# Attention outputs of a head kept and normed four blocks at a time, convolution taps given out one by one, the gate projected last, the query copies on ScalarE

## The chip, the core and the metric

The kernel runs on one core of one Trainium2 chip. The metric is the time of one execution in device microseconds (us). The core has TensorE (PE in the profile, PEld for its weight loads), VectorE (DVE), ScalarE (ACT) and GpSimd (POOL); SyncE (SP) issues the DMAs. The engines run their own instruction lists in order and meet only at semaphores.

## What is computed

One layer of a hybrid decoder on 1024 tokens and 16 meta tokens, model width 1024, in float32. The normed input is projected once, and three groups use it: differential attention (4 heads), a short gated convolution and a Mamba-2 scan (4 groups of 4 heads). The parts of the reference that the change touches:

```python
u = rmsnorm(h, norm_w[layer])
proj = jnp.einsum('bld,de->ble', u, w_in[layer])
(q, k, v, g_attn, c_b, c_c, c_h, g_conv, z, xbc, dt) = jnp.split(proj, IN_SPLIT_POINTS, axis=-1)
y_attn = diff_attention_branch(q, k, v, ...) * jax.nn.silu(g_attn)
y_conv = short_conv_branch(c_b, c_c, c_h, sconv_w[layer]) * jax.nn.silu(g_conv)
y_ssm = ssd_branch(z, xbc, dt, ...)
h = h + jnp.einsum('ble,ed->bld', concat(y_attn, y_conv, y_ssm), w_out[layer])

# in diff_attention, a block of 128 queries of one head, two maps m = 0, 1
s = jnp.einsum('bqhmd,bkhmd->bhmqk', qi, k) * scale
p = jax.nn.softmax(jnp.where(mask, s, MASK_VALUE), axis=-1)
a = p[:, :, 0] - lam * p[:, :, 1]
o = jnp.einsum('bhqk,bkhe->bqhe', a, v)
# and after it
o = rmsnorm(o, sub_norm_w) * (1.0 - lam_init)
```

## The kernel before

The work is done head by head. A loop runs over heads 0 to 2 (`BODY`), head 3 is written out (`LAST`), and a prologue (`AHEAD`) norms the input and projects the first head's q, k and v. After the heads come the output projection (L1360) and the final norm.

**Projections.** A head has 14 weight tiles of 128 columns (`TILES`): q, k, v, the attention gate (TG), the convolved tiles xs 0, xs 1, B and C (TXS0, TXS1, TB, TC), two z tiles, and four of the short convolution (TCB, TCC, TCH, TGC). Float32 is kept by splitting each weight and input into a high and a low part: three matmuls for each product (high by high, high by low, low by high; L1353). A tile is loaded by SP ("load"), copied to its high part by ScalarE (L807) and its low part made by GpSimd (L738), both in step "split"; two tiles, TZ1 and TCB (`SHARED`), have their low part made half by GpSimd and half by VectorE (L1097). A tile is projected in three pieces of 348 columns, each in two halves of 12 matmuls. Pieces go in turn to two banks of PSUM, and a bank is used again when the engine that empties it gives it back (`bank_free`).

**Order.** All engines walk through one list of steps, written by `schedule()`. Each engine takes from it the steps in which it has a part, so the list sets the order of every engine. Step s of the attention stage (s = 0 to 8) does for block s: scores of map 0, exponential, scores of map 1, exponential, mix. In the same step it does for block s-1: "turn" (TensorE transposes the mixed probabilities, VectorE and ScalarE copy them back), "values" (times v) and "o_norm". "attn_out" is for block s-2. Between them `fill()` gives out half pieces of projections as cover.

**A block's output before.** VectorE scales and clips the 128x128 result into `o_n` (L1200, L1201). ScalarE sums its squares (L908), VectorE makes the mean (L1205, L1206), GpSimd the power -1/2 (L725), VectorE the normed block (L1208). TensorE transposes it, and VectorE multiplies it with the gate (L1212, which gives `attn_ok`). `o_n` has room for one block, and the turn of the next block waits for the last of these:

```python
eng.wait_ge(a_m_ok, it * QB + a + 1)
eng.wait_ge(attn_ok, it * QB + a + 1)
for n in range(a + 1):
    turn(t_ps[n // 4][:, ...], prob[0][:, ...])
```

**Taps.** The four convolved tiles get four taps each on VectorE (L1157, three times L1159), a tanh on ScalarE (L882) and a gate on VectorE (L1168). The `half_pieces()` function puts each at a fixed half piece after its tile. The parameters of a head are gathered by ten small VectorE operations (L1105 to L1117) with the first convolved tile.

**Queries.** ScalarE scales the two high parts out of PSUM (L852, L853). VectorE subtracts them from the product (L1127, L1129) and copies each high part to the other half of the partitions (L1128, L1130). The second copy gives the bank back.

Of the kernel before, what the change touches and what calls it, by code (L numbers as in the profile page):

```python
# [15 lines left out]
P = 128  # L16
D = 1024
T = 1024
META = 16
# [31 lines left out]
(TQ, TK, TV, TG, TXS0, TXS1, TB, TC, TZ0, TZ1, TCB, TCC, TCH, TGC) = range(NT)  # L51
# [23 lines left out]
def half_pieces(tiles, d):  # L75
# [3 lines left out]
    tail = [[] for _ in range(6)]  # L79
    places = units + tail  # L80
    n = 0
    for t in tiles:
# [8 lines left out]

        if TXS0 <= t <= TC:
            for tap in range(4):
                places[n - 1 + tap].append(("taps", (t, tap), d))
            places[n + 3].append(("gate_taps", t, d))
        if t == TGC:
            for part in range(5):
                places[n - 1 + part].append(("conv", part, d))
    return units, tail
# [44 lines left out]
def schedule(last):  # L144

# [8 lines left out]
    def ahead(name, t, d):  # L154
        add(name, t % NT, d + t // NT)

    def filler(units, slots):
# [8 lines left out]
        return fill  # L166

    def emit(unit):
        for name, arg, d in unit:
            if name in ("load", "split"):  # L170
                ahead(name, arg, d)
            else:
                add(name, arg, d)


    units, tail = half_pieces([TG, TXS0, TXS1, TB, TC], 0)
    units[-1] += [("split", TZ1, 0), ("load", TCB, 0), ("load", TCC, 0)]
    fill = filler(units, sum(ATT_FILL))
    for s in range(QB + 1):
        f = [ATT_FILL[s] * w for w in ATT_SPLIT]  # L180
# [15 lines left out]
        if s >= 1:  # L196
            add("values", s - 1)
        if s < QB:
            add("mix", s)
        if s >= 1:  # L200
            add("o_norm", s - 1)
        fill(f[2])

    emit(tail[0])
    add("z", 1)
    emit(tail[1])
    add("z", 2)
    emit(tail[2])
    emit(tail[3])
    add("z", 3)  # L210
    add("attn_out", QB - 1)
    add("store_attn")
    add("z", 4)
# [1385 lines left out]
```

## Time and profile before

| | |
|---|---|
| runs of the kernel before | 1181.78 us median of 3 (1181.15 to 1184.64) |
| the profiled execution: its own time | 1181.38 us |
| its span, first to last instruction | 1179.7 us |
| mean granted TensorE clock | 0.985 |
| TensorE busy | 1086.4 us, 92% |
| VectorE busy | 647.6 us, 55% |
| ScalarE, GpSimd busy | 381.9 us, 32%; 293.0 us, 25% |

A granted clock of 1.0 is 2.4 GHz and 0.5 is 1.2 GHz. The rows of matmuls overlap: one lasts until its result is written, while the next starts well before. In the rows further down, `[1.22 <-DVE y_a L1208]` means that the engine was idle for 1.22 us before this instruction, and that line 1208 of VectorE ended the wait.

### The profile page before, as it was taken

To read this page: it belongs to the slowest core of one execution; us is meant where nothing else is said; L and a number is where in the kernel's file an instruction comes from. 1 tells how busy PE (TensorE), PEld (TensorE's weight loads), DVE (VectorE), ACT (ScalarE), POOL (GpSimd) and SP (SyncE) were. 2 spreads that over 40 slices of the span, in tenths; PEclk is the share of its full clock that TensorE was granted. 3 is DMA by queue.
4 is the path that set the end of the run, shared out by engine and by line. 5 is a ranking of instruction groups with operands and counts; after the bars stand their busy time and mean duration, and the time that the engine had idled before them with its cause. 6 is when DMAs were issued, how large, how long until landed. Compare 5 with 4: busy or idle time off the path is not lost.

```text
span 1179.7 us, 18700 instructions
## 1 busy us (share of the span) xinstructions
PE 1086.4 (92%) x6681; PEld 1002.8 (85%) x6681; DVE 647.6 (55%) x1329; ACT 381.9 (32%) x840; POOL 293.0 (25%) x255
## 2 busy tenths in 40 slices
PE   4889989999999899998998999999989998999997
PEld 3679888899888889998888899999888997888885
DVE  6453666645546766465467664654675646325324
ACT  5223333232333332233333322333332324323324
POOL 5311120332211203331112033311121332432433
PEclk9989999999999999999999999999999999999999
DMA  5101001311130013111300131112011222963423
GB/s 185 36 22 55 18 20 36 90 46 45 54 91 19 20 35 99 41 41 54 91 18 20 35 99 41 41 54 90 19 36 55 74 80 79 343 226 122 157 80 143
DMA packets 91876, 85.89 MB, mean 73 GB/s; under 512 B 4478, under 2 KB 78316, under 8 KB 91788
## 3 DMA queue, kind: packets, MB, share of 16 engines
q1 hardware_dynamic: 91788, 84.70, 22.6%
q8 instruction: 57, 0.93, 0.3%
q14 instruction: 31, 0.25, 0.1%
HBM read 72.03 MB, written 12.66 MB: 72 GB/s over the span
## 4 chain that ended last, share of the span: by engine, by line
PE 43%; issue 35%; DVE 8%; POOL 8%; DMA 2%; ACT 2%; SPq 1%; POOLq 0%; DVEq 0%; ACTq 0%
PE ps L1353 19%; PE ps L1360 15%; POOL w_lo L738 5%; PE ps L1515 3%; PE ps L1345 2%; POOL small L725 2%; DMA acum_b<-acum_scratch 2%; PE ps L1529 1%; DVE lm_buf L1231 1%; DVE work L1159 1%; PE ps L1531 1%; PE ps L1535 1%; ACT w_hi L807 1%; DVE work L1188 1%; DMA work<-in_x 1%
## 5 line engine op out<-in xcount | busy, mean ns | idle before, releaser
L1353 PE MATMUL ps<-u_hi,w_hi 128*128 128x348 f32 x1152 | 393.6, 342 | 22.9 <-DVE q_hl L1130 14.7
L1353 PE MATMUL ps<-u_lo,w_hi 128*128 128x348 f32 x1152 | 375.0, 326 | 0.0
L1353 PE MATMUL ps<-u_hi,w_lo 128*128 128x348 f32 x1152 | 374.2, 325 | 0.0
L1353 PEld LDWEIGHTS ps<-u_hi,w_hi 128*128 128x128 f32 x1152 | 221.4, 192 | 32.3 <-issue 11.2
L1353 PEld LDWEIGHTS ps<-u_lo,w_hi 128*128 128x128 f32 x1152 | 220.9, 192 | 0.7
L1353 PEld LDWEIGHTS ps<-u_hi,w_lo 128*128 128x128 f32 x1152 | 220.5, 191 | 0.0
L738 POOL TENSOR_TENSOR w_lo<-w_raw,w_hi 128x1024 fp32r<-128x1024 f32 (+1 forms) x56 | 129.2, 2308 | 190.5 <-ACT w_hi L807 190.5
L725 POOL TENSOR_TENSOR small<-small,m_half 128x1 f32<-128x1 f32 (+1 forms) x81 | 54.6, 674 | 463.4 <-DVE small L1206 294.9
L1360 PE MATMUL ps<-w_hi,u_hi 128*128 128x512 f32 x256 | 99.8, 390 | 4.2 <-DVE u_lo L996 3.3
L1360 PE MATMUL ps<-w_hi,u_lo 128*128 128x512 f32 x256 | 101.6, 397 | 0.0
L1360 PE MATMUL ps<-w_lo,u_hi 128*128 128x512 f32 x256 | 101.4, 396 | 0.0
L1345 PE MATMUL ps<-ident,work 128*128 128x128 f32 (+2 forms) x401 | 64.3, 298 | 36.3 <-DVE conv_u L1212 19.1
L996 DVE TENSOR_TENSOR u_lo<-q_hl,u_hi 128x1024 fp32r<-128x1024 f32 x32 | 43.0, 1348 | 88.2 <-ACT u_hi L791 88.1
L1180 DVE TENSOR_REDUCE small<-ps 128x1 f32<-128x144 f32 (+7 forms) x64 | 49.5, 774 | 71.7 <-PE ps L1466 67.9
L1345 PEld LDWEIGHTS ps<-ident,work 128*128 128x128 f32 (+2 forms) x401 | 49.7, 149 | 44.5 <-issue 32.6
L729 POOL TENSOR_TENSOR w_lo<-w_raw,w_hi 128x512 fp32r<-128x512 f32 x32 | 59.1, 1853 | 106.6 <-ACT w_hi L795 106.5
L1515 PE MATMUL ps<-w_hi,u_hi 128*128 128x256 f32 x256 | 74.0, 289 | 6.1 <-DVE w_lo L1097 3.8
L1515 PE MATMUL ps<-w_lo,u_hi 128*128 128x256 f32 x256 | 71.9, 281 | 0.0
L1515 PE MATMUL ps<-w_hi,u_lo 128*128 128x256 f32 x256 | 71.8, 280 | 0.0
L896 ACT ACTIVATE work<-ps,small 128x144 f32<-128x144 f32 (+7 forms) x64 | 48.0, 749 | 66.1 <-DVE small L1180 66.1
L791 ACT CAST u_hi<-q_hl 128x1024 fp32r<-128x1024 f32 x32 | 33.5, 1051 | 99.1 <-PE ps L1360 84.3
L1360 PEld LDWEIGHTS ps<-w_hi,u_hi 128*128 128x128 f32 x256 | 49.1, 192 | 16.1 <-issue 5.0
(209 smaller groups left out, 1693.4 us busy)
## 6 DMA issues: line engine op xcount, KB each, us to landing
w_raw<-in_w_in SPq DMA_DIRECT2D x56, 512.0 KB, 3.9
q_hl<-y_scratch SPq DMA_DIRECT2D x32, 512.0 KB, 3.7
acum_b<-acum_scratch SPq DMA_DIRECT2D x32, 256.0 KB, 4.0
w_raw<-in_w_out SPq DMA_DIRECT2D x32, 256.0 KB, 4.3
work<-in_x SPq DMA_DIRECT2D x8, 512.0 KB, 3.8
y_scratch<-ys SPq DMA_DIRECT2D x8, 512.0 KB, 3.3
work<-in_x SPq DMA_DIRECT2D x4, 1024.0 KB, 8.8
out<-work SPq DMA_DIRECT2D x8, 512.0 KB, 3.0
```

The lines of the kernel that those rows point to most:

```text
L725: return eng.tensor_tensor(to[0:rows_, n:n + 1], of[0:rows_, n:n + 1], m_half[0:rows_, :], ALU.pow)
L729: eng.tensor_tensor(wo_lo[:, b, :], wo_raw[:, b, :], wo_hi[:, b, :].bitcast(F32), ALU.subtract).then_inc(wo_lo_ok, 1)
L738: eng.tensor_tensor(w_lo[:, a % 2, ks, :], w_raw[:, a % 2, ks, :], w_hi[:, a % 2, ks, :].bitcast(F32), ALU.subtract).then_inc(w_lo_ok, 1)
L791: eng.copy(y_hi[:, b, :], y_raw[:, b, :]).then_inc(y_hi_ok, 1)
L807: eng.copy(w_hi[:, b, :, :], w_raw[:, b, :, :]).then_inc(w_hi_ok, 1)
L896: eng.activation(prob[m][:, 0:nk], s_ps[:, 0:nk], ACT.Exp, bias=mx[:, m:m + 1], accum_out=psum_e[:, s % 2, m:m + 1]).then_inc(exp_ok, 1)
L996: eng.tensor_tensor(y_lo[:, b, :], y_raw[:, b, :], y_hi[:, b, :].bitcast(F32), ALU.subtract).then_inc(y_lo_ok, 1)
L1180: eng.tensor_reduce(mx[:, m:m + 1], s_ps[:, 0:nk], AX.X, ALU.max, negate=True).then_inc(max_ok, 1)
L1345: return eng.transpose(dst, src, ident[0:n, 0:n])
L1353: ins = eng.matmul(dst, w[:, k, 0:m], u[:, k, cols], start=(k == 0 and n == 0), stop=(k == KD - 1 and n == 2))
L1360: ins = eng.matmul(ps[:, t, :], y[:, b, t * P:(t + 1) * P], w[:, b, :], start=(first and m == 0), stop=(last and m == 2), skip_group_check ...
L1515: ins = eng.matmul(pb[p % 2][:, 0:GW], u[:, k, ca:cb], w[:, :, k, :], start=(k == 0 and n == 0), stop=(k == KD - 1 and n == 2))
```

## The change

- **Attention outputs.** `o_n` has room for eight blocks (it lies in `conv_y`, which is free during attention). Steps "o_norm" and the eight "attn_out" go. Instead "o_mean" and "o_scale" treat four blocks in one operation each, after blocks 3 and 7. Two "attn_out" steps transpose four blocks into a bank of their own and gate 512 columns at once; the first stands behind the last turn, the second behind z 3. The turn of a block waits for `o_c_ok`, the clip of the block before, and no longer for `attn_ok`.
- **Order of tiles.** The gate tile TG comes after TC, so the parameters move to the first step of a head.
- **Taps.** Taps, gates of tiles and the five steps of the short convolution go to a list, `jobs`. `spare()` gives out one job at a place, at three places of each step.
- **Shared low halves.** For TZ1 and TCB ScalarE copies the high part in two halves. VectorE makes the first low half as soon as the first is there and GpSimd the second. TensorE waits for the second only at its second half of work.
- **Query copies.** ScalarE makes them; the bank is given back after VectorE's second subtraction. The first scores wait for `q_twice_ok`.
- **Meta rows.** `a_meta` and `v_meta` have 128 rows, zero below the 16 in use, so the last matmul of "values" has 128 rows too.

```diff
-TILES = [(C_Q, P), (C_K, P), (C_V, P), (C_G, P), (C_XS, GW), (C_XS + P, GW), (C_B, P), (C_C, P),
+TILES = [(C_Q, P), (C_K, P), (C_V, P), (C_XS, GW), (C_XS + P, GW), (C_B, P), (C_C, P), (C_G, P),
...
         if TXS0 <= t <= TC:
-            for tap in range(4):
-                places[n - 1 + tap].append(("taps", (t, tap), d))
-            places[n + 3].append(("gate_taps", t, d))
+            jobs += [(n, ("taps", (t, tap), d)) for tap in range(4)] + [(n, ("gate_taps", t, d))]
...
+                while jobs and jobs[0][0] <= state[0] - 7:
+                    emit([jobs.pop(0)[1]])
                 emit(units[state[0]])
                 state[0] += 1
...
+        def spare(n):
+            while n > 0 and jobs and jobs[0][0] <= state[0]:
+                emit([jobs.pop(0)[1]])
+                n -= 1
+        return fill, spare
...
         if s < QB:
             add("scores", (s, 0))
-        if s >= 2:
-            add("attn_out", s - 2)
         fill(f[0])
+        if s < QB:
+            spare(ATT_SPARE[0])
...
+        if s == QB:
+            add("split", TZ1)
+            add("load", TCB)
+            add("load", TCC)
+            add("attn_out", 0)
...
-        if s >= 1:
-            add("o_norm", s - 1)
+        if s == 6:
+            add("o_scale", 0)
         fill(f[2])
...
-ATT_SPLIT = (.3, .3, .4)
+ATT_SPLIT = (.2, .4, .4)
+ATT_LAST = (1, 0, 0)
+ATT_SPARE = (1, 1, 1)
+SCAN_SPARE = (1, 1, 1)
...
@@ ScalarE @@
+                        if a in SHARED:
+                            eng.copy(w_hi[:, b, 0:KD // 2, :], w_raw[:, b, 0:KD // 2, :]).then_inc(w_half_ok, 1)
+                            eng.copy(w_hi[:, b, KD // 2:KD, :], w_raw[:, b, KD // 2:KD, :]).then_inc(w_hi_ok, 1)
...
                             eng.mul(q_hi[1][QK:P, to], src[QK:P, of], QK ** -0.5).then_inc(qk_hi_ok, 1)
+                            eng.wait_ge(qk_hi_ok, it * 2 * PIECES + tc + 1)
+                            eng.copy(q_hi[0][QK:P, to], q_hi[0][0:QK, to].bitcast(F32))
+                            eng.copy(q_hi[1][0:QK, to], q_hi[1][QK:P, to].bitcast(F32)).then_inc(q_twice_ok, 1)
...
@@ VectorE @@
-                            eng.tensor_copy(q_hi[0][up, to], q_hi[0][lo, to].bitcast(F32))
...
-                            eng.tensor_copy(q_hi[1][lo, to], q_hi[1][up, to].bitcast(F32)).then_inc(done, 1)
...
+                    elif step == "o_scale":
+                        ns = slice(4 * a, 4 * a + 4)
+                        eng.wait_ge(o_rs_ok, it * 2 + a + 1)
+                        own(eng, eng.tensor_tensor(o_rs[:, ns], o_rs[:, ns], o_fit[:, ns], ALU.mult))
+                        eng.tensor_tensor(o_n[:, ns, :], o_n[:, ns, :], o_rs[:, ns].unsqueeze(2).to_broadcast([P, 4, P]), ALU.mult).then_inc(o_n_ok, 1)
                     elif step == "attn_out":
+                        eng.wait_ge(o_tr, it * 2 + a + 1)
+                        cols = slice(META + 4 * P * a, META + 4 * P * (a + 1))
+                        eng.scalar_tensor_tensor(gate[:, cols], ot_ps[a][:, :], a_norm[:, 0:1], gate[:, cols],
...
@@ TensorE @@
-                        eng.wait_ge(attn_ok, it * QB + a + 1)
+                        eng.wait_ge(o_c_ok, it * QB + a + 1)
```

The first place is VectorE's list around step 5 of a head, before: the mean and norm of block 4 (L1205 to L1208), two taps (L1159), the reduction of the next scores (L1180), the gate of block 3 (L1212) and a third tap.

```order
L1205 TENSOR_SCALAR small<-small 128x1
L301 REGISTER_ALU
L1206 TENSOR_SCALAR small<-small 128x1
L1208 TENSOR_SCALAR y_a<-y_a,small 128x128
L1159 SCALAR_TENSOR_TENSOR work<-lm_buf,par_cw,work 128x1044
L301 REGISTER_ALU
L1159 SCALAR_TENSOR_TENSOR work<-lm_buf,par_cw,work 128x1044
L301 REGISTER_ALU
L1176 REGISTER_ALU
L1180 TENSOR_REDUCE small<-ps 128x1
L1212 SCALAR_TENSOR_TENSOR conv_u<-ps,a_norm,conv_u 128x128
L1159 SCALAR_TENSOR_TENSOR work<-lm_buf,par_cw,work 128x1044
```

The same step in the changed kernel, from its mix of block 5 (L1206) on: a tap (L1177), the reduction (L1198), a tap, and the copy of the turned probabilities (L1211).

```order
L1206 SCALAR_TENSOR_TENSOR work<-work,small 128x784
L1177 SCALAR_TENSOR_TENSOR work<-work,par_cw 128x1044
L307 REGISTER_ALU
L1194 REGISTER_ALU
L1198 TENSOR_REDUCE small<-ps 128x1
L1177 SCALAR_TENSOR_TENSOR work<-work,par_cw 128x1044
L307 REGISTER_ALU
L1210 REGISTER_ALU
L1211 COPY conv_g<-ps 128x512
```

Norm and gate of a block have left this place, and the taps stand one at a time between the operations of the softmax.

The second place is VectorE's list for the first query piece of the next head, before: subtraction, copy, subtraction, copy, then a step of the short convolution (L1220).

```order
L1126 ISA
L1127 SCALAR_TENSOR_TENSOR q_hl<-ps,q_hl 64x332
L1128 CAST q_hl<-q_hl 64x332
L1129 SCALAR_TENSOR_TENSOR q_hl<-ps,q_hl 64x332
L1130 CAST q_hl<-q_hl 64x332
L1220 SCALAR_TENSOR_TENSOR conv_y<-conv_u,par_sw,conv_y 128x1024
```

The changed kernel's list there, with the second piece's subtractions and then the convolution step (L1244).

```order
L1146 ISA
L1147 SCALAR_TENSOR_TENSOR q_hl<-ps,q_hl 64x332
L1148 SCALAR_TENSOR_TENSOR q_hl<-ps,q_hl 64x332
L1146 REGISTER_ALU
L1147 SCALAR_TENSOR_TENSOR q_hl<-ps,q_hl 64x348
L1148 SCALAR_TENSOR_TENSOR q_hl<-ps,q_hl 64x348
L1244 SCALAR_TENSOR_TENSOR conv_y<-conv_u,par_sw,conv_y 128x1024
```

The copies have gone to ScalarE, and the convolution step stands a piece later.

The third place is VectorE's list at the start of a head, before: the reduction of the first scores and then the copy of the turned values (L1171).

```order
L1180 TENSOR_REDUCE small<-ps 128x1
L1170 REGISTER_ALU
L1171 COPY conv_b_s<-ps 128x512
L1137 ISA
L1138 ISA
L1139 SCALAR_TENSOR_TENSOR conv_u<-th_piece,ps 128x348
```

The changed kernel's list there, from the last of the small parameter operations to the copy of the turned values (L1189).

```order
L1134 COPY small<-d_bc 128x4
L1135 REGISTER_ALU
L1135 COPY sg<-stat 128x180
L307 ISA
L1137 MEMSET lm_buf 128x3
L307 REGISTER_ALU
L1188 REGISTER_ALU
L1189 COPY conv_b_s<-ps 128x512
L1194 REGISTER_ALU
L1198 TENSOR_REDUCE small<-ps 128x1
```

The parameters stand ahead of that copy now, and the gate's product (L1139) has left this place.

## Rows read from the trace of the kernel before

**Rows 1.** The page, part 1: busy time, share and count of each engine

```profile
PE 1086.4 (92%) x6681; PEld 1002.8 (85%) x6681; DVE 647.6 (55%) x1329; ACT 381.9 (32%) x840; POOL 293.0 (25%) x255
```

**Rows 2.** TensorE's waits: us in total, times, longest

```profile
PE ps L1345 <- DVE conv_u L1212: 19.1, 13, 2.0
...
PE ps L1345 <- DVE y_a L1208: 8.0, 16, 1.2
...
PE ps L1353 <- DVE q_hl L1130: 14.7, 7, 5.5
...
PE ps L1515 <- DVE w_lo L1097: 3.8, 3, 1.3
...
PE ps L1353 <- POOL w_lo L738: 3.4, 3, 1.1
```

**Rows 3.** Timeline, head 1, step 5: start us, us, engine, line

```profile
389.11 2.37 POOL L738 TENSOR_TENSOR w_lo<-w_raw,w_hi 128x1024 fp32r<-128x1024 f32 x1
389.18 2.38 DVE L1208 TENSOR_SCALAR y_a<-y_a,small 128x128 f32<-128x128 f32 x1 [0.67 <-POOL small L725]
...
391.62 0.33 PE L1345 MATMUL ps<-ident,y_a 128*128 128x128 f32 x1 [1.22 <-DVE y_a L1208]
...
393.36 0.32 PE L1353 MATMUL ps<-u_lo,w_hi 128*128 128x348 f32 x1
...
393.52 0.32 PE L1353 MATMUL ps<-u_hi,w_lo 128*128 128x348 f32 x1
...
395.33 0.34 DVE L1212 SCALAR_TENSOR_TENSOR conv_u<-ps,a_norm,conv_u 128x128 f32<-128x128 f32 x1
...
395.82 0.96 PE L1345 MATMUL ps<-ident,work 128*128 128x128 f32 x7 [1.98 <-DVE conv_u L1212]
```

**Rows 4.** Timeline, head 2's query pieces, end of head 1's pass

```profile
527.98 2.62 POOL L738 TENSOR_TENSOR w_lo<-w_raw,w_hi 128x1024 fp32r<-128x1024 f32 x1 [1.56 <-ACT w_hi L807]
...
528.73 0.50 DVE L1127 SCALAR_TENSOR_TENSOR q_hl<-ps,q_hl 64x332 fp32r<-64x332 f32 x1 [0.37 <-ACT q_hl L853]
...
529.24 1.55 DVE L1128 CAST q_hl<-q_hl 64x332 fp32r<-64x332 f32 x1
...
530.16 0.46 ACT L853 ACTIVATE q_hl<-ps 64x348 fp32r<-64x348 f32 x1
...
531.71 0.43 PE L1353 MATMUL ps<-u_hi,w_hi 128*128 128x348 f32 x1 [1.83 <-DVE q_hl L1130]
```

**Rows 5.** Windows of 3.4 us: PE, PEld, DVE, ACT, POOL, clock, DMA; two of six

```profile
161.50:164.90 3.40, 3.40 (x15) 3.32 (x14) 1.30 (x3) 2.49 (x5) 0.00 (x0) 0.50 0.00 0
...
769.10:772.40 3.30, 3.30 (x14) 3.30 (x13) 3.10 (x6) 0.00 (x0) 0.00 (x0) 0.50 0.00 0
```

**Rows 6.** Timeline, parameters in head 0, then the start of head 2

```profile
112.02 2.16 DVE L1105 COPY par_cw<-par 128x8 f32 x1
...
115.04 0.06 DVE L1117 MEMSET lm_buf<- 128x3 f32 x1
...
566.10 2.39 POOL L738 TENSOR_TENSOR w_lo<-w_raw,w_hi 128x1024 fp32r<-128x1024 f32 x1 [6.51 <-ACT w_hi L807]
...
569.15 0.69 DVE L1171 COPY conv_b_s<-ps 128x512 f32<-128x512 f32 x1 [2.68 <-PE ps L1345]
```

**Rows 7.** Timeline, the split and z 1 of head 1

```profile
428.64 1.77 DVE L1097 TENSOR_TENSOR w_lo<-w_raw,w_hi 128x512 fp32r<-128x512 f32 x1
...
430.53 0.38 PE L1515 MATMUL ps<-w_hi,u_hi 128*128 128x256 f32 x1 [1.26 <-DVE w_lo L1097]
```

**Rows 8.** Groups by line: busy us, mean ns, idle before (taps, gates, tanh, exponential)

```profile
L1159 DVE SCALAR_TENSOR_TENSOR work<-lm_buf,par_cw,work 128x1044 f32<-128x1044 f32 x24 | 31.2, 1299 | 0.1
...
L1168 DVE SCALAR_TENSOR_TENSOR work<-th_tile,work 128x1044 f32<-128x1044 f32 x16 | 19.9, 1243 | 11.9 <-ACT th_tile L882 11.9
...
L896 ACT ACTIVATE work<-ps,small 128x144 f32<-128x144 f32 (+7 forms) x64 | 48.0, 749 | 66.1 <-DVE small L1180 66.1
...
L882 ACT ACTIVATE th_tile<-work 128x1044 f32<-128x1044 f32 x16 | 17.0, 1065 | 7.1 <-DVE work L1159 7.1
```

More of the change, by code:

```diff
@@ L45 @@
 C_Z, C_XS, C_B, C_C, C_DT = 4096, 5120, 6144, 6656, 7168
-TILES = [(C_Q, P), (C_K, P), (C_V, P), (C_G, P), (C_XS, GW), (C_XS + P, GW), (C_B, P), (C_C, P),
+TILES = [(C_Q, P), (C_K, P), (C_V, P), (C_XS, GW), (C_XS + P, GW), (C_B, P), (C_C, P), (C_G, P),
          (C_Z, GW), (C_Z + P, GW), (C_CB, P), (C_CC, P), (C_CH, P), (C_GC, P)]
 NT = len(TILES)
-(TQ, TK, TV, TG, TXS0, TXS1, TB, TC, TZ0, TZ1, TCB, TCC, TCH, TGC) = range(NT)
+(TQ, TK, TV, TXS0, TXS1, TB, TC, TG, TZ0, TZ1, TCB, TCC, TCH, TGC) = range(NT)
 SHARED = (TZ1, TCB)
@@ L78, in half_pieces @@
     units = [[] for _ in range(len(tiles) * PIECES * 2)]
-    tail = [[] for _ in range(6)]
-    places = units + tail
+    jobs = []
     n = 0
@@ L92, in half_pieces @@
         if TXS0 <= t <= TC:
-            for tap in range(4):
-                places[n - 1 + tap].append(("taps", (t, tap), d))
-            places[n + 3].append(("gate_taps", t, d))
+            jobs += [(n, ("taps", (t, tap), d)) for tap in range(4)] + [(n, ("gate_taps", t, d))]
         if t == TGC:
-            for part in range(5):
-                places[n - 1 + part].append(("conv", part, d))
-    return units, tail
+            jobs += [(n, ("conv", part, d)) for part in range(5)]
+    return units, jobs
 def ahead():
@@ L152, in add, with emit, filler @@
             out.append((name, arg, d))
-    def ahead(name, t, d):
-        add(name, t % NT, d + t // NT)
-    def filler(units, slots):
+    def emit(unit):
+        for name, arg, d in unit:
+            if name in ("load", "split"):
+                add(name, arg % NT, d + arg // NT)
+            else:
+                add(name, arg, d)
+    def filler(units, jobs, slots):
         state = [0, 0.0]
@@ L163, in fill @@
             while state[0] < len(units) and state[0] < len(units) * state[1] / slots - 1e-9:
+                while jobs and jobs[0][0] <= state[0] - 7:
+                    emit([jobs.pop(0)[1]])
                 emit(units[state[0]])
                 state[0] += 1
[L166 to L178, printed above, removed]
+        def spare(n):
[3 more added lines that the diff above has]
+        return fill, spare
+    units, jobs = half_pieces([TXS0, TXS1, TB, TC, TG], 0)
+    fill, spare = filler(units, jobs, sum(ATT_FILL))
     for s in range(QB + 1):
-        f = [ATT_FILL[s] * w for w in ATT_SPLIT]
+        f = [ATT_FILL[s] * w for w in (ATT_SPLIT if s < QB else ATT_LAST)]
         if s < QB:
             add("scores", (s, 0))
-        if s >= 2:
-            add("attn_out", s - 2)
         fill(f[0])
+        if s < QB:
+            spare(ATT_SPARE[0])
         if s == 0:
@@ L218, in schedule @@
     units += [[]] * PAUSE
-    conv, tail = half_pieces([TCB, TCC, TCH, TGC], 0)
+    conv, jobs = half_pieces([TCB, TCC, TCH, TGC], 0)
+    jobs = [(n + len(units), job) for n, job in jobs]
     if last:
@@ L230, in schedule @@
     else:
-        more = half_pieces([TQ, TK, TV], 1)[0]
-        for n, unit in enumerate(tail):
-            more[n] += unit
-        tail = []
-        units += conv + more
+        units += conv + half_pieces([TQ, TK, TV], 1)[0]
     slots = LAST_FILL if last else SCAN_FILL
-    fill = filler(units, sum(slots))
+    fill, spare = filler(units, jobs, sum(slots))
     for c in range(1, CH + 3):
@@ L450, in build @@
         cmix = few(1)
-        o_ss = few(1)
-        o_ms = few(1)
-        o_fit = few(1)
-        o_rs = few(1)
+        o_ss = few(QB)
+        o_ms = few(QB)
+        o_fit = few(QB)
+        o_rs = few(QB)
         z_ss = few(2)
@@ L1513, in iteration @@
                         for k in range(KD):
+                            if a == 1 and k == KD // 2:
+                                eng.wait_ge(w_lo_ok, it * NT + TZ1 + 3)
                             for n, (u, w) in enumerate(terms):
```

120 lines of the change are left out of this document (69 added, 51 removed).

## The prediction

> **What bounds the kernel now.** I read the page's table of busy time first. TensorE is busy for 92% of the span and every other engine for at most 55% [rows 1], so only TensorE's waits are worth anything, along with the time it spends at the lower clock. The second view is TensorE's list of waits. Two of its causes belong to attention's output path. It waited 19.1 us in 13 waits for L1212, the gating of an attention block, and 8.0 us in 16 waits for L1208, the norm of a block. It waited 14.7 us in 7 waits for L1130, the second of VectorE's two query copies. Waits for the low weight halves (L1097, L738) make 3.8 and 3.4 us [rows 2].
>
> Third, the timeline of one stretch of head 1 shows how the first two arise. GpSimd starts its 2.37 us split of a weight tile at 389.11. VectorE's norm of 128x128 starts at 389.18 and ends with it, 2.38 us later. TensorE's turn of that block goes at 391.62, idle for 1.22. VectorE then has two taps and a reduction in front of L1212 (395.33 to 395.67), and TensorE's next turn starts at 395.82, idle for 1.98 [rows 3]. So one block of 128 tokens passes VectorE, GpSimd, VectorE, TensorE and VectorE again before TensorE may turn the next block's probabilities.
>
> The idle time understates a wait. Two projections start 0.16 us apart (393.36, 393.52), but each row is 0.32 long [rows 3], so after a row ends TensorE is already 0.16 late. I add 0.16 to each wait.
>
> **Removed from the attention stage.** The turn of block s now waits only for the clip of block s-1 (o_c_ok), which VectorE does a whole step earlier. The transposes of finished outputs go out in two lots of four, long after their scaling. All 29 waits go: 19.1 + 8.0 + 29 x 0.16 = 31.7 us. The lower bound of this gain is 22, if a third of them come back as others. VectorE also loses eight small norms for two of four blocks; that is no gain by itself, since it is not the bound.
>
> **Query copies.** Before, the bank is given back after L1127, L1128, L1129, L1130. In the row's case the copy L1128 took 1.55 us, beside GpSimd's split (527.98 to 530.60), and TensorE started at 531.71 after 1.83 idle. The subtraction before it took 0.50 [rows 4]. Now the bank is free after two subtractions: 528.73 + 2 x 0.51 = 529.75. TensorE would have come at 531.71 - 1.83 - 0.16, which is 529.72, so at most 0.1 is left. Of the 14.7 us [rows 2], 5.5 is a single wait ahead of the heads, behind a long VectorE chain, and only its two copies go there (0.7 us, an estimate from 0.33 each for uncontended ones). The other six waits go whole: 9.2 + 6 x 0.16 = 10.2. Together 10.9 us.
>
> ScalarE gets two copies of about 0.45 us per piece, the price of L853 on the same shape [rows 4]. That is 0.9 us, behind which stand the sum of squares, the store of an SSM block and the next weight copy. ScalarE is busy 32% [rows 1], and the scores that need the copies come two tiles later, each of them three pieces of 24 projections at 0.16. I cost it at nothing. Uncovered it would be 12 x 0.9 = 11 us.
>
> **Clock.** TensorE's granted clock falls to 0.5, which is 1.2 GHz against 2.4, for about 3.4 us in six stretches inside the heads. The first starts at 161.5 and the last at 769.1 [rows 5]. Three come right after the second L1212 wait of a pair like the one in rows 3, the other three right after an L1130 wait. At half clock 3.4 us does 1.7 us of work; I take 1.5, since the edges are not whole. If the waits before them go, the stretches should go: 6 x 1.5 = 9.0 us. The bounds are 0 and 10.2.
>
> **Gate last, low halves exchanged.** The split of TZ1 costs a wait per head before z 1: VectorE's half took 1.77 us and TensorE started at 430.53 [rows 7], 3.8 us in three heads [rows 2], and about as much in the fourth. ScalarE now copies the half in two parts and VectorE takes the first, so z 1 can start about 0.5 us sooner. But the change also takes away a half piece (1.9 us) that stood between the last turn and its values. Four transposes remain as cover (0.4 us) against a copy of about 0.7 us on VectorE and two on ScalarE: a new wait of about 0.5. Net I take 0.7 x 4 = 2.8 us; bounds -2 and 5. For TCB, TensorE's first half no longer waits for GpSimd. The three L738 waits of L1353 [rows 2] are this one: 3.4 + 3 x 0.16 = 3.9 us.
>
> Gains together: 31.7 + 10.9 + 9.0 + 2.8 + 3.9 = 58.3 us.
>
> **What it costs.** First, the parameters' ten small operations move from step 2 of a head to just after its first reduction. There GpSimd's split runs (566.10 to 568.49), and the first of these copies took 2.16 us beside such a split, the rest 0.92 (114.18 to 115.10). They would end at 568.49 + 0.92 = 569.41, where the copy of the turned values starts now at 569.15 [rows 6]. Behind that stand ScalarE's half of the copy, the first exponential and the second scores. So 0.3 us each, 1.2 in all; without the split 0.
>
> The Trainium skill, page SBUF — State Buffer, section Who interferes with whom, states that VectorE and GpSimd share a port pair which whoever starts first holds for a whole instruction. It names copies, tensor_scalar and operations with two SBUF inputs as VectorE's users of it. The 2.38 of L1208 against 2.37 of the split agrees with it.
>
> Second, taps (1.30 us) and tile gates (1.24 us) [rows 8] now stand one at a time ahead of mix, of the turn's copy or of a reduction. Mostly TensorE has a half piece or two (1.9 us each) there. The tight places are steps 3 and 5: the gate of a tile waits for ScalarE's tanh and stands ahead of the copy of the turned probabilities, with one half piece as cover. The tanh takes 1.07 us and an exponential 0.75 on average [rows 8], with small copies between them: about 2.2 against 1.9, so 0.3 us each. The rest of the 1.5 us per head that I take is for taps that meet a split. That is 6.0 us, with bounds 0 and 20 (one whole tap and three gates per head). Third, in the last head a second convolution step now precedes the first low half of the output stage, for which TensorE waits. It is the same operation as a tap over 1024 columns, about 1.3 us [rows 8], a part of it beside ScalarE's copy ahead of that half: 1.0 us, with bounds 0 and 1.3. Costs together: 8.2.
>
> The sum is against the profiled execution's own 1181.38 us: 1181.4 - 58.3 + 8.2 = 1131.3. The median of the runs is 1181.78, 0.4 us above, which changes nothing, so I predict **1131 us**.
>
> **Rivals.**
> - *The forecast*, 1120 to 1140: chance 0.70. For it speak the five lower engines, idle nearly half the time or more. Against it, these are chains, not loads.
> - *New waits on the softmax path.* A tap and a split of a weight tile fall ahead of mix in most steps, so that TensorE waits for mix or for the second scores. At 5 us per head instead of 1.5 that is 14 us more: 1145, up to 1160. VectorE's operation held for 2.38 us [rows 3] speaks for it; that TensorE never waited for mix before speaks against. Chance 0.17. By the page named above it would take a hold of 2.4 us at two places of each head.
> - *The clock stretches stay* where they are, since something other than the waits causes them: 1131 + 9 = 1140. In the last head the same pair of waits was followed by none, which speaks for it. Chance 0.07.
> - *The change does not do what it says*: the waits are taken over one for one by others, the exponential first, and the time is 1179 to 1185. Chance 0.03.
> - *Slower.* VectorE's convolution work, given out singly, stands in TensorE's path whole. A head has 16 taps at 1.30 at most and 4 gates at 1.24: 25.8 us, 103 in four heads, less the 58 gained gives 1226. It decides once more than 56% of that work is uncovered. VectorE is idle 45% of the time [rows 1], and the cover of 1.9 us exceeds any single operation. Chance 0.03.
>
> **How the numbers follow.** A measurement of this kernel can tell about 0.3% from no change. Faster: 0.70 + 0.17 + 0.07 = 0.94, and 0.01 of the case of one-for-one waits, so 0.95. Same 0.02. Slower 0.03. The range must leave out no more than 2 in 10: it starts at 1118, where the taps cost nothing and all six clock stretches give their 1.7, with a few more waits gone. It ends at 1152, in the middle of the second rival.
>
> **What would show it.** TensorE's waits for the two lines of the attention output and for the query copies are gone. The granted clock in the heads is 1.0 throughout. A wait of about 0.5 stands before the values of block 7, and about 1 us more before the output stage. The wait at TCC's third piece and the one at the loop's return stay. The prediction is wrong if TensorE's list gets a new line, for mix, for the exponential or for the turn's copy, of more than 10 us in all; or if half-clock stretches stand elsewhere in the heads.

## The result, and the profile after

The changed kernel takes 1112.19 us (median of 4 runs, 1107.86 to 1114.32), against 1181.47 us before on the same chip. The ratio is 0.9407, 95% interval [0.937, 0.9445]. It is faster, as predicted, but the time lies below the predicted range of 1118 to 1152. The profiled execution took 1113.45 us.

The span of the changed kernel is 1111.7 us, and its table of busy time is:

```profile
PE 1061.7 (96%) x6681; PEld 993.4 (89%) x6681; DVE 612.4 (55%) x1217; ACT 394.5 (35%) x872; POOL 289.0 (26%) x233
```

Beside [rows 1] this line splits the gain. TensorE's idle time (span less busy) was 1179.7 - 1086.4 = 93.3 us and is 1111.7 - 1061.7 = 50.0, so 43.3 less. But TensorE also became 24.7 us less *busy* with the same 6681 matmuls. Together they are the 68.0 us by which the span fell. Of the prediction's 58.3 us of gains only 15.1 were of the second kind: 9.0 for the clock and 38 late starts of 0.16 us.

TensorE's waits after (us in total, times, longest):

```profile
PE ps L1377 <- DVE q_hl L1148: 6.6, 2, 4.8
...
PE ps L1384 <- DVE u_lo L1016: 4.3, 1, 4.3
...
PE ps L1491 <- issue: 1.7, 1, 1.7
PE ps L1491 <- ACT work L916: 1.6, 2, 1.3
PE ps L1513 <- ACT a_meta L923: 1.4, 3, 0.5
```

All lines of [rows 2] are gone but the one for the query pieces (L1148 now). Of its 6.6 us, 4.8 is the wait ahead of the heads. L1016 is the start of the output stage. The waits at L1491, for the scores of a head's first block, are 4.5 us in four (one of them, of 1.3, for a line not shown); the kernel before had 2.4 us in two of that kind (L1462). New are the small waits for the values of block 7: 1.4 us in three at this line, and a fourth of 0.5 for the copy of the turned probabilities in the last head. No line is there for a tap or for mix.

The windows of the changed kernel (PE, PEld, DVE, ACT, POOL, clock, DMA), at its half-clock stretches behind the prologue and ahead of the final norm:

```profile
498.10:501.50 3.40, 3.40 (x14) 3.40 (x13) 2.72 (x4) 0.07 (x1) 0.50 (x1) 0.50 0.00 0
921.40:928.20 6.80, 4.78 (x11) 3.84 (x12) 6.57 (x7) 1.29 (x4) 1.52 (x1) 0.50 0.01 2
```

One of the six stretches inside the heads [rows 5] has a successor (498.1). A longer one, 6.8 us, is new at the output stage. TensorE was busy for 4.78 us of it and still waiting for the rest, so it costs 2.4 us and not 3.4.

The end of "values" in head 1, after: the last full matmul, the matmul of the meta rows (two rows of the trace), and the next projection:

```profile
387.63 0.28 PE L1513 MATMUL ps<-conv_b_s,conv_g 128*128 128x128 f32 x1
387.74 0.39 PE L1514 MATMUL ps<-v_meta,a_meta 128*128 128x128 f32 x2
387.89 0.41 PE L1377 MATMUL ps<-u_hi,w_hi 128*128 128x348 f32 x1
```

The same place in the kernel of the first experiment, which differs from the changed one only in giving this matmul 16 rows:

```profile
391.75 0.28 PE L1513 MATMUL ps<-conv_b_s,conv_g 128*128 128x128 f32 x1
391.96 0.48 PE L1514 MATMUL ps<-v_meta,a_meta 16*128 16x128 f32 x2
392.37 0.43 PE L1377 MATMUL ps<-u_hi,w_hi 128*128 128x348 f32 x1
```

With 128 rows the projection starts 0.15 us behind the pair's start, with 16 rows 0.41 us. From the start of the last full matmul it is 0.26 against 0.62; over all 32 places the medians are 0.254 and 0.618. The kernel before, with its 16 rows, has the 0.618 too (in head 1 from 404.15 to 404.76). This happens 32 times, which makes 11.6 us, and no view calls it a wait. It is a cost inside TensorE's busy time.

### The profile page after: what moved, and what is told of

It is laid out like the page before. It is cut to its first block, busy times and chain, and to the rows that moved or that the text cites. A ratio compares the mean times of both kernels' runs of the same rounds, so it can differ in the third digit from the quotient of the medians.

```text
span 1111.7 us, 18631 instructions
## 1 busy us (share of the span) xinstructions
PE 1061.7 (96%) x6681; PEld 993.4 (89%) x6681; DVE 612.4 (55%) x1217; ACT 394.5 (35%) x872; POOL 289.0 (26%) x233
## 4 chain that ended last, share of the span: by engine, by line
PE 89%; DVE 5%; issue 3%; ACT 1%; SPq 1%; DMA 1%; DVEq 0%; POOLq 0%; POOL 0%; ACTq 0%
PE ps L1377 48%; PE ps L1384 16%; PE ps L1548 8%; PE ps L1369 4%; PE ps L1513 3%; PE ps L1562 2%; PE ps L1491 2%; PE ps L1492 2%; PE ps L1564 1%; PE ps L1568 1%; DVE lm_buf L1255 1%; PE ps L1514 1%; PE ps L1533 1%; DMA work<-in_x 1%; PE ps L1495 0%
## 5 line engine op out<-in xcount | busy, mean ns | idle before, releaser
L1377 PE MATMUL ps<-u_hi,w_hi 128*128 128x348 f32 x1152 | 389.2, 338 | 11.0 <-DVE q_hl L1148 6.6
L1377 PEld LDWEIGHTS ps<-u_hi,w_hi 128*128 128x128 f32 x1152 | 218.5, 190 | 14.8 <-issue 5.5
L1377 PEld LDWEIGHTS ps<-u_lo,w_hi 128*128 128x128 f32 x1152 | 218.4, 190 | 0.8
L1377 PEld LDWEIGHTS ps<-u_hi,w_lo 128*128 128x128 f32 x1152 | 218.0, 189 | 0.0
L738 POOL TENSOR_TENSOR small<-small,m_half 128x1 f32<-128x1 f32 (+2 forms) x57 | 47.2, 829 | 220.6 <-DVE small L1313 129.0
L1198 DVE TENSOR_REDUCE small<-ps 128x1 f32<-128x144 f32 (+7 forms) x64 | 49.5, 773 | 96.2 <-PE ps L1495 95.0
L1016 DVE TENSOR_TENSOR u_lo<-q_hl,u_hi 128x1024 fp32r<-128x1024 f32 x32 | 42.0, 1317 | 92.0 <-ACT u_hi L804 92.0
L916 ACT ACTIVATE work<-ps,small 128x144 f32<-128x144 f32 (+7 forms) x64 | 48.0, 750 | 68.1 <-DVE small L1198 68.1
```

Source lines behind the costliest of these rows:

```text
L738: return eng.tensor_tensor(to[0:rows_, n:n + w], of[0:rows_, n:n + w], m_half[0:rows_, 0:w], ALU.pow)
L916: eng.activation(prob[m][:, 0:nk], s_ps[:, 0:nk], ACT.Exp, bias=mx[:, m:m + 1], accum_out=psum_e[:, s % 2, m:m + 1]).then_inc(exp_ok, 1)
L1016: eng.tensor_tensor(y_lo[:, b, :], y_raw[:, b, :], y_hi[:, b, :].bitcast(F32), ALU.subtract).then_inc(y_lo_ok, 1)
L1198: eng.tensor_reduce(mx[:, m:m + 1], s_ps[:, 0:nk], AX.X, ALU.max, negate=True).then_inc(max_ok, 1)
L1377: ins = eng.matmul(dst, w[:, k, 0:m], u[:, k, cols], start=(k == 0 and n == 0), stop=(k == KD - 1 and n == 2))
```

## The experiments

Idle is TensorE's span less its busy time, as above. Span, busy and idle are of the profiled execution. The ratio is to runs of the kernel before that were taken along with each group of experiments; their medians are 1182.35 (1 to 4), 1185.63 (5 to 8) and 1183.76 us (9 to 12), against 1181.47 with the changed kernel. So a difference of up to about 4 us between medians of different groups shows nothing by itself.

One more number is needed to compare spans: half of the time for which TensorE was busy at half clock is lost. By the traces this loss is 13.37 us before and 8.64 in the changed kernel; in experiments 1 to 12 it is 6.8, 15.4, 6.6, 5.6, 41.0, 16.6, 12.0, 7.1, 6.3, 8.4, 6.0 and 7.4. A part of it lies in the prologue (3.1 us before, 4.5 in the changed kernel), which no edit here touches but for the query pieces, and it varies there from 1.7 to 4.5.

| kernel | median us | ratio to before | span | busy | idle |
|---|---|---|---|---|---|
| before | 1181.47 | | 1179.7 | 1086.4 | 93.3 |
| changed | 1112.19 | 0.9407 [0.937, 0.9445] | 1111.7 | 1061.7 | 50.0 |
| 1 changed, 16 rows | 1124.37 | 0.9496 [0.946, 0.9533] | 1123.0 | 1071.2 | 51.8 |
| 2 before, 128 rows | 1187.41 | 1.0023 [1.0, 1.0046] | 1182.9 | 1077.9 | 105.0 |
| 3 before, outputs kept | 1146.3 | 0.9683 [0.9646, 0.9719] | 1141.3 | 1074.9 | 66.4 |
| 4 before, query copies on ScalarE | 1166.78 | 0.9855 [0.9818, 0.9892] | 1164.3 | 1080.2 | 84.1 |
| 5 changed, taps in a bunch | 1220.88 | 1.0313 [1.0281, 1.0344] | 1214.0 | 1093.7 | 120.3 |
| 6 changed, gate first | 1134.39 | 0.9573 [0.9544, 0.9602] | 1133.3 | 1067.5 | 65.8 |
| 7 changed, query copies on VectorE | 1123.51 | 0.9484 [0.9454, 0.9513] | 1121.5 | 1064.3 | 57.2 |
| 8 changed, convolution late | 1110.89 | 0.9376 [0.9348, 0.9404] | 1107.0 | 1059.9 | 47.1 |
| 9 before with 2, 3 and 4 | 1129.05 | 0.9545 [0.9511, 0.9578] | 1122.1 | 1064.3 | 57.8 |
| 10 changed, taps at fixed places | 1114.45 | 0.9416 [0.938, 0.9451] | 1111.8 | 1061.5 | 50.3 |
| 11 changed, halves as before | 1117.21 | 0.9437 [0.9404, 0.9469] | 1115.6 | 1061.3 | 54.3 |
| 12 changed, 8 and parameters late | 1112.25 | 0.939 [0.9362, 0.9419] | 1110.9 | 1059.7 | 51.2 |

### 1. The meta matmul with 16 rows again

```diff
-eng.matmul(o_ps[:, P:2 * P], a_meta[:, :], v_meta[:, :], start=False, stop=True).then_inc(o_done, 1)
+eng.matmul(o_ps[:, P:2 * P], a_meta[0:META, :], v_meta[0:META, :], start=False, stop=True).then_inc(o_done, 1)
```

> The changed kernel with one edit: the last matmul of values reads only the 16 rows in use of a_meta and v_meta again. Theory A (a 16-row contraction between 128-row ones holds TensorE): the trace of before has 0.618 us from the last full matmul of values to the next projection, the changed kernel 0.254, so 0.364 x 32 = 11.6 us more, about 1124 against 1112. Theory B (the prediction's own view, which gave this edit no price): the missing 18 us came from elsewhere and this kernel stays at 1112.

Measured: 1124.37 us, 12.2 more than the changed kernel; the span is 11.3 longer, 0.35 us for each of 32 blocks. Of it 9.5 us is busy time and 1.8 idle. Theory A is confirmed: 11.6 us by the starts, 1.9 for one more late query piece, less 1.9 for a smaller loss at half clock, make 11.6, against the 11.3 of the spans. The edit that the prediction gave no price is worth as much as the query copies.

From the last full matmul on, the starts follow one another at 0.205, 0.214 and 0.200 us with 16 rows, and at 0.112, 0.112 and 0.031 with 128 (medians of the 32 places). The middle step lies between the two rows of the meta matmul itself.

The Trainium skill, page TensorEngine Tiling (Array Packing), section Key Properties, states that a change of tiling mode (not only of the tile) drains TensorE. The rows above fit that only in part, and only if a matmul of 16 rows among ones of 128 is such a change, which the page doesn't say: the middle step is dearer by 0.10 us too, though both of its rows have 16. So the 11.6 us are shown to come from the row count; why they do is not shown.

### 2. The kernel before with 128 rows

```diff
-v_meta = y_a[0:META, 0:P]
-a_meta = sb("a_meta", [META, P])
+a_meta = sb("a_meta", [P, P])
+v_meta = sb("v_meta", [P, P])
...
+eng.memset(a_meta[:, :], 0.0).then_inc(consts, 1)
+eng.memset(v_meta[:, :], 0.0).then_inc(consts, 1)
```

> The kernel before with one edit: a_meta and v_meta have 128 rows with zeros below the 16 in use, and the last matmul of values has 128 rows. Theory A: 11.6 us less, about 1170, and the waits of attention's output path stay at 27 us. Theory B: 1181, unchanged.

Measured: no gain, 1187.41 us (ratio 1.0023, interval from 1.0 to 1.0046). Theory A, 1170, is wrong. Theory B has the number, but not because the edit saves nothing. Its waits of TensorE (L1214 and L1210 are the L1212 and L1208 of [rows 2]):

```profile
PE ps L1347 <- DVE conv_u L1214: 22.8, 16, 2.1
...
PE ps L1347 <- DVE y_a L1210: 14.8, 20, 1.6
```

The step from the last full matmul to the next projection is 0.254 us here too, 11.6 us saved. Busy time fell by 8.5 us; the loss at half clock grew by 2.1 and there are seven more of the two kinds of waits, 1.1 us of late starts. The two waits grew from 27.1 to 37.6. In the kernel before, a block's output had to pass VectorE and GpSimd before the next turn. TensorE came to that wait sooner and stood there longer. So the same edit gains nothing in the kernel before, and 11.3 us in the changed one, where the outputs are kept.

### 3. The kernel before with the outputs kept

```diff
...
+        if s == QB:
+            add("attn_out", 0)
...
-        if s >= 1:
-            add("o_norm", s - 1)
+        if s == 6:
+            add("o_scale", 0)
...
-                        eng.wait_ge(attn_ok, it * QB + a + 1)
+                        eng.wait_ge(o_c_ok, it * QB + a + 1)
```

> The kernel before with the kept outputs alone (norm, turn and gate four blocks at a time, the turn waits for the clip); order of tiles, taps in their old places, query copies, halves and meta rows as before. The prediction's term: 27.1 us of waits and their 29 x 0.16 go, 31.7 us, and three stretches at the lower clock with them, 4.5: about 1145. Rival: with the taps still in bunches TensorE waits for mix or for the turn's copy instead, and half of it is left: about 1163.

Measured: 1146.3 us, span 38.4 us shorter. Idle fell by 26.9, where the two waits of [rows 2] had been 27.1. Busy fell by 11.5: 29 x 0.16 = 4.6 for the late starts behind the waits, and four half-clock stretches fewer in the heads (those at 287.9 and 738.4 are left), at 1.7 each 6.8. The expectation, 1145, is met, and its rival is refuted.

### 4 and 7. The query copies alone, there and back

Experiment 4 is the kernel before with this edit; experiment 7 takes it out of the changed kernel.

```diff
@@ ScalarE @@
+eng.wait_ge(qk_hi_ok, it * 2 * PIECES + tc + 1)
+eng.copy(q_hi[0][QK:P, to], q_hi[0][0:QK, to].bitcast(F32))
+eng.copy(q_hi[1][0:QK, to], q_hi[1][QK:P, to].bitcast(F32)).then_inc(q_twice_ok, 1)
@@ VectorE @@
-eng.tensor_copy(q_hi[0][up, to], q_hi[0][lo, to].bitcast(F32))
...
-eng.tensor_copy(q_hi[1][lo, to], q_hi[1][up, to].bitcast(F32)).then_inc(done, 1)
```

> The kernel before with the query copies on ScalarE alone. The prediction's term: 10.9 us of waits go and three stretches at the lower clock with them, 4.5: about 1166. Rival, since one wait for L1148 of 1.8 us with its half-clock stretch is left in the changed kernel: the subtractions are late instead in some heads, and a third of it is left, about 1171.

> The changed kernel with the query copies back on VectorE. The prediction's term: 10.9 us of waits come back and up to three half-clock stretches of 1.5 us: 1123 to 1128. Rival: the convolution's steps stand two pieces later now, so the copies meet less in front of them, and half of it comes back: 1118.

Measured: 1166.78 us, span 15.4 us shorter than before; and 1123.51, 11.3 us above the changed kernel. Both expectations are met. In experiment 4 one half-clock stretch of six is left in the heads, the one in the prologue at 45.5 is gone, and one of 3.4 us is new at the output stage (977.3). In experiment 7 the wait for the query pieces is back, 12.2 us in five waits (L1146).

ScalarE, with 12 pieces more to copy, makes TensorE wait nowhere for them. The copies were rightly costed at nothing.

### 5 and 10. Where the taps stand

```diff
-ATT_SPARE = (1, 1, 1)
+ATT_SPARE = (9, 9, 9)    # experiment 5
```

```diff
-            jobs += [(n, ("taps", (t, tap), d)) for tap in range(4)] + [(n, ("gate_taps", t, d))]
+            for tap in range(4):
+                units[n - 1 + tap].append(("taps", (t, tap), d))
+            units[n + 3].append(("gate_taps", t, d))    # experiment 10
```

The 9 lets a tile's five jobs go out together.

> The changed kernel, but a tile's four taps and its gate are given out together at the first place where they may go (nine jobs at a place instead of one), ahead of the turn's copy or of mix. Theory A (giving them out singly is what keeps TensorE free): the five in a row take 4 x 1.30 + 1.24 = 6.4 us against 1.9 to 3.8 us of cover, so 3 us of wait for each of 16 tiles, 48 us: about 1160. Theory B (once a block's output is off the path any placement is covered): 1112 to 1116.

> The changed kernel with the four taps and the gates' product of a tile bound to the fixed half pieces that they had before, instead of being taken from a list when VectorE has time to spare. Theory 1 (taps spread over half pieces cost little wherever they stand, only all five in one place cost 40): 1112 to 1116. Theory 2 (the list is what took them out of TensorE's way): 1120 to 1130, with new waits of TensorE for the values or the scores behind a tap.

Measured: 1220.88 and 1114.45. Waits of TensorE in experiment 5:

```profile
PE ps L1493 <- ACT work L916: 50.3, 15, 4.8
PE ps L1371 <- DVE work L1206: 18.4, 4, 4.6
```

Four taps and a gate in a row (4 x 1.30 + 1.24 = 6.4 us by [rows 8]) hold up the reduction and with it the exponential (L916), or mix (L1206). Idle rises by 70.3. Busy time rises by 32.0 too: the granted clock falls to 0.96 of full on average, and the loss at half clock rises by 32.4. Theory A had the mechanism, but with 48 us less than half of the 108.7 measured: it had the waits at 3 us for each tile, and left out the clock. Spread out, no tap shows in TensorE's list of waits, and whether by a list or at fixed half pieces makes 2.3 us or less (theory 1). This holds even though taps do meet splits. The first of the two groups of taps at this line in the changed kernel, durations in ns as least, median and most, then first and last start:

```profile
L1177 DVE SCALAR_TENSOR_TENSOR work<-work,par_cw x24: 1293/1299/3445, 114.1 to 805.9; 128x1044 f32<-128x1044 f32 x24
```

The usual tap takes 1.30 us as in [rows 8]. One in each head took 3.44, beside a split by GpSimd (149.37 to 152.31 in head 0), and TensorE waited for none of them.

In experiments 5, 6 and 10 VectorE's product of the attention output with the gate also waits until the PSUM banks of the gate's last pieces have been given back, which keeps the order right there.

### 6. The gate first again

```diff
-TILES = [(C_Q, P), (C_K, P), (C_V, P), (C_XS, GW), (C_XS + P, GW), (C_B, P), (C_C, P), (C_G, P),
+TILES = [(C_Q, P), (C_K, P), (C_V, P), (C_G, P), (C_XS, GW), (C_XS + P, GW), (C_B, P), (C_C, P),
...
-    units, jobs = half_pieces([TXS0, TXS1, TB, TC, TG], 0)
+    units, jobs = half_pieces([TG, TXS0, TXS1, TB, TC], 0)
```

> The changed kernel with the old order of tiles, the gate tile ahead of the convolved ones; taps still singly. The parameters move back to step 2. The prediction's terms for the order: the wait at z 1 is kept small by the exchanged halves, the wait before the second scores of a head's first block (1.3 us in head 0) goes, and the taps of the last tile crowd the z pieces: 1112 to 1116. Rival: the gate last is what frees the z stage, and TensorE waits 1 us or more at each of z 2, z 3 and the first chunk: 1124 or more.

Measured: 1134.39 us, 22.2 above the changed kernel (the span 21.6). The rival has the size; it named waits at z 2, z 3 and the first chunk, and only the one at the first chunk is there. The line of these waits, and the timeline ahead of the first of the four, of 4.85 us, which ends at 197.07:

```profile
PE ps L1371 <- DVE work L1186: 19.3, 4, 4.9
```

```profile
190.58 3.98 DVE L1177 SCALAR_TENSOR_TENSOR work<-lm_buf,par_cw,work 128x1044 f32<-128x1044 f32 x3
...
195.70 1.25 DVE L1186 SCALAR_TENSOR_TENSOR work<-th_tile,work 128x1044 f32<-128x1044 f32 x1 [1.14 <-ACT th_tile L902]
```

With the gate first, tile C's three last taps, tanh and gate all stand ahead of the scan's first chunk, which needs them. A half-clock stretch of 6.8 us goes with each of the four waits, and costs 2.3 to 3.0 us, since it begins while TensorE still waits. So listed taps and the gate's place belong together. The prediction costed the order only at z 1.

### 8 and 12. Two small edits on the changed kernel

```diff
-        spare(SCAN_SPARE[2])
+        spare(SCAN_SPARE[2] if not (last and c >= CH) else 0)    # experiments 8 and 12
```

```diff
-            units[n].append(("params", 0, d))
+            units[n + 4].append(("params", 0, d))                    # experiment 12
```

> The changed kernel, but in the last head the convolution's second step stands behind the start of the output stage, as before. Theory A (the extra 1.0 us of wait in front of the output stage, 4.3 against 3.3, is what lets TensorE's clock fall to 0.5 for 6.8 us there, while before it stayed at 1.0): the wait is 3.3 again, the half-clock stretch goes, 1.0 + 3.4 = 4.4 us less, about 1108. Theory B (the stretch comes by itself): 1.0 less, 1111.

> The changed kernel with two small edits: in the last head the convolution's later steps stand behind the output stage's start (as in the run before), and the head's parameters are worked out two pieces (four half pieces) later, so that they do not run beside the split on the pair of ports that VectorE and GpSimd share and the first scores of a head do not wait for them. Theory 1 (both are on TensorE's path): 1.0 for the output stage, and 1 to 1.3 for the wait of the first head's scores, so 1109 to 1110, which is less than the scatter of the runs can tell from 1112; what tells is the trace, where the wait of 1.26 at the first scores is gone. Theory 2 (the parameters are late in their new place): the first scores of a head wait for the softmax's inputs in all four heads, 1115 or more.

Measured: 1110.89 and 1112.25 us, neither to be told from 1112.19, so the 1109 to 1110 expected for experiment 12 did not show. In experiment 8 the wait at the output stage is 3.3 us instead of 4.3, but the half-clock stretch there stays (917.1): theory B. In experiment 12 the wait is 3.3 as well, and that stretch is not there. The wait for the second scores in head 0 is gone too, and still its span is 3.9 us longer than that of 8. Its timeline, where GpSimd's split meets VectorE's product of two operands in SBUF ahead of the query pieces:

```profile
494.69 2.39 POOL L751 TENSOR_TENSOR w_lo<-w_raw,w_hi 128x1024 fp32r<-128x1024 f32 x1 [1.57 <-ACT w_hi L824]
494.69 2.66 DVE L1307 TENSOR_TENSOR y_n<-y_a,work 128x256 f32<-128x256 f32 x1 [0.18 <-DVE y_a L1303]
```

The same two in experiment 8:

```profile
492.84 2.68 POOL L751 TENSOR_TENSOR w_lo<-w_raw,w_hi 128x1024 fp32r<-128x1024 f32 x1 [1.56 <-ACT w_hi L824]
492.84 0.43 DVE L1307 TENSOR_TENSOR y_n<-y_a,work 128x256 f32<-128x256 f32 x1 [0.18 <-DVE y_a L1303]
```

Both pairs start in the same hundredth of a microsecond. In the one, VectorE takes 2.66 us; L1148 is late and TensorE waits 1.77. In the other VectorE takes 0.43 and GpSimd is the longer, and TensorE does not wait. In experiment 12 GpSimd won in three heads (waits of 1.75, 1.77 and 1.76 us), in the changed kernel's profiled execution in one, in experiment 8 in none. Three waits of about 1.9, with their late starts, are 5.8 us, more than both edits gave. Neither theory had named this one. In experiments 6 and 11 VectorE's product starts 0.05 us ahead of the split in three heads each, and it takes 0.42 or 0.43 us in all six.

### 9 and 11. What is left when the big parts are in

> The kernel before with three parts of the change together: a head's attention outputs kept and normed four at a time, the query copies on ScalarE, and the last matmul of values over 128 rows. Left out are the new order of the tiles (gate last), the taps given out singly and the other half of the shared tile's split. Theory 1 (the parts add up): 1182 - 36 (kept) - 15.6 (query copies) - 11.6 (128 rows, now that no wait for VectorE swallows them) = 1119, range 1115 to 1123; the rest of the change is then worth about 7. Theory 2 (the parts overlap: the same waits were counted twice): 1130 or more, and the rest of the change is worth 18 or more.

> The changed kernel with the halves of the tiles that GpSimd and VectorE split between them as they were before (VectorE takes the upper half and waits for the whole rounding; z's second tile is waited for whole). Theory 1 (the waits for z1, 2.8 net over the heads, and for C's second tile, 3.9, come back): 1115 to 1120. Theory 2 (with the gate projected last, C is no longer late, and only z1's waits come back): 1112 to 1115. In both the trace shows them as waits of TensorE for the low halves.

Experiment 9 is the kernel before with the edits of 2, 3 and 4 together. Experiment 11, in the split of a shared tile:

```diff
-                        ks = slice(0, KD // 2)
-                        eng.wait_ge(w_half_ok, it * len(SHARED) + SHARED.index(a) + 1)
+                        ks = slice(KD // 2, KD)
+                        eng.wait_ge(w_hi_ok, it * NT + a + 1)
```

Measured: 1129.05 us for the three parts together, 10 above where they add up, at the edge of theory 2. The profiled spans say the same: 1179.7 - 38.4 - 15.4 - 11.3 = 1114.6, against 1122.1. The losses at half clock account for most of it: against before they are 6.8 us less in experiment 3 and 7.8 less in 4, and the 11.3 of experiment 1 holds 1.9 of the other sign, 12.7 together; experiment 9 lost only 7.1 less. The other 1.9 is the late query piece that is in the 11.3 of experiment 1. Together these are 7.5. So what overlaps is the clock's part. The idle times add up, 93.3 - 26.9 - 9.2 = 57.2 by experiments 3 and 4, against 57.8.

Undoing the shared halves costs 5.0 us (span 3.9): theory 1. Its waits for the low halves are 5.2 us in seven, with their late starts 6.3. The split of z 1, first in experiment 9, then in experiment 11:

```profile
180.25 1.26 POOL L746 TENSOR_TENSOR w_lo<-w_raw,w_hi 128x512 fp32r<-128x512 f32 x1 [16.11 <-ACT w_hi L815]
...
180.29 1.77 DVE L1108 TENSOR_TENSOR w_lo<-w_raw,w_hi 128x512 fp32r<-128x512 f32 x1
```

```profile
180.00 0.69 DVE L1112 TENSOR_TENSOR w_lo<-w_raw,w_hi 128x512 fp32r<-128x512 f32 x1 [1.02 <-ACT w_hi L819]
...
180.05 1.78 POOL L750 TENSOR_TENSOR w_lo<-w_raw,w_hi 128x512 fp32r<-128x512 f32 x1 [13.84 <-ACT w_hi L819]
```

Here too the one that starts later, by 0.04 or 0.05 us, takes 1.77 instead of 0.69 or 1.26. TensorE's wait for z 1 was 1.71 us in the first case and 0.54 in the second. In the changed kernel the two overlap by only 0.13 us (VectorE 181.74 to 182.43, GpSimd from 182.30 in 1.27) and there is no wait. The spans of experiments 9 and 11 differ by 6.5 us; z 1's waits, 6.4 us against 2.1, are 4.3 of it, and three waits for the key pieces, which experiment 11 has not, are 1.7.

The Trainium skill, page SBUF — State Buffer, section Who interferes with whom, calls the port pair that VectorE and GpSimd share an exclusive lock, names a VectorE instruction with two SBUF inputs as one that contends with a GpSimd instruction that reads SBUF, and states that issue order decides who blocks. The two pairs of experiments 9 and 11 agree, one in each direction. In the two pairs of experiments 12 and 8 one of the two is held as well, but their rows do not tell the order.

## Why the prediction was right or wrong

The sum was 58.3 gained less 8.2 lost, 50.1 us; the span fell by 68.0. By kind:

| | forecast | by the two traces |
|---|---|---|
| waits, with 0.16 for each | 41.1 | 43.3 + 47 x 0.16 = 50.8 |
| half clock | 9.0 | 13.37 - 8.64 = 4.7 |
| the meta matmul's rows | none | 32 x 0.364 = 11.6 (experiment 1: 11.3) |
| sum | 50.1 | 67.1 of 68.0 |

The waits of TensorE between its instructions number 72 before and 25 after (gaps over 0.1 us), so 47 fewer. In the second row the five stretches gone from the heads give 8.5 us; the new one at the output stage takes 2.4 of it and the prologue 1.4.

- **The step that failed: "Meta rows" had no term.** It stood in the list of changes, and the prediction gave it neither a gain nor a reason for none. The starts in the trace of the kernel before held one half of the price, 0.618 us from the last full matmul of values to the next projection; the other half, 0.254 with 128 rows, no run had shown yet. Experiment 1 measured 11.3 us. With it the sum would have been 1120, inside the range. Of the 7.8 us that are left, the taps are 6.0 and other waits 3.7, against 4.3 that the clock gave less; the other 2.4 have no cause shown.
- **The attention stage (31.7): right.** Experiment 3 gave 38.4, of which 26.9 + 4.6 = 31.5 is this term. Both mechanisms of [rows 3] are gone.
- **Query copies (10.9): nearly right.** Alone they gave 15.4 with their stretches, in the changed kernel 11.3 if taken back (the span 9.8). The list of waits went from 14.7 to 6.6, not to 4.8; the rest is the wait of 1.77 at 497.13, behind a product of VectorE that took 2.66 us beside a split (493.48).
- **Clock (9.0): mis-sized, 4.7.** Five of the six stretches went with their waits, which refutes the rival in which all stay. One came back behind the 1.77 wait at 497.13, so the clock in the heads is not 1.0 throughout, as the prediction had it. The one at the output stage was not foreseen. Experiment 8 shortened the wait ahead of it from 4.3 to 3.3 us and did not remove it; experiment 12 and the kernel before have the same wait of 3.3 and no such stretch. So the length of that wait does not decide it, and what does stays open.
- **Gate last and halves (2.8 + 3.9).** The halves alone gave 3.9 to 5.0 (experiment 11). TCB was right: three waits of 1.02 in experiment 11 (there called C's second tile) against none. At z 1 it also counted which engine came first to the shared ports, and not only the 0.5 us of an earlier start. The new wait ahead of the values of block 7 is 0.48 in each head, forecast about 0.5. That listed taps need the gate to come last (22 us in experiment 6) was missed; it did not touch the sum, since the change has both.
- **Taps and gates singly (6.0): mis-sized, nothing.** The place that was priced, ahead of the turn's copy, never made TensorE wait. That "the cover of 1.9 us exceeds any single operation" was a misreading: the trace of the kernel before already had one tap in each head of 3.31 us, beside a split. It did no harm, but the 1.30 us "at most" is the usual time and no bound. Spread out, nothing near the bound of 20 was seen; in a bunch they cost over 100.
- **Parameters (1.2): right in size, not in place.** They met the split in head 0 (2.34 us for one), which gave a wait of 1.26 us for the second scores, and another of 0.30 in head 2; both are gone in experiment 12, where the parameters come later. **Convolution ahead of the output stage (1.0): right,** 4.33 against 3.3.

## What to carry to other kernels

Look for savings in TensorE's busy time as well as in its waits: a matmul of 16 rows among ones of 128 cost 0.36 us here and stands in no list of waits. Give every edit on the list of changes a term, even if it is zero with a reason. A saving in busy time is worth something only once the chain that TensorE waits for is out of its way: the same edit gave nothing before and 11 to 12 us after. Spread long VectorE work over the places between the short operations that TensorE needs: here the single operation was covered, five in a row were not.

## What the runs showed of the hardware

- With 16 rows instead of 128, the last matmul of a block's values (two rows of the trace) put off the next projection's start from 0.254 to 0.618 us behind the last full matmul, and 32 blocks cost 11.3 us.
- VectorE and GpSimd at their shared ports: with starts equal to 0.01 us, either may be the one held (0.43 us for VectorE and 2.68 for GpSimd, or 2.66 and 2.39). Repeated runs of the changed kernel spread over 6.5 us (1107.86 to 1114.32). Where VectorE is held, TensorE waits 1.77 us, so up to three such waits may be a part of the spread; only one execution has a trace, and it was not shown. The clock is not what tells the fastest run from the slowest: both have a mean granted clock of 0.993.
- The half-clock stretch does not follow from the wait's length alone. In experiment 12 the wait of 1.77 us at 498.34 was followed by 3.4 us at half clock (from 499.8) and one of 1.79 at 310.84, for the first scores, by another (from 312.1); the waits of 1.75 at 280.34 and of 1.76 at 715.54 were followed by none. The 3.3 us ahead of the output stage went without one before and in experiments 3 and 12, with 3.4 us at half clock in 2 and 4, and with 6.8 in 8 and 9.
